# Two mixer streams in one steady interleave, modulation sums as a third stream, and low parts moved from GpSimd to VectorE

## The reference, cut to what matters

```python
for l in range(DEPTH):                                   # DEPTH = 2
    mod = cond @ ada_w[l] + ada_b[l]                     # six vectors of 1024
    sh1, sc1, g1, sh2, sc2, g2 = split(mod, 6)
    h = _rms_norm(x, norm1_g[l]) * (1.0 + sc1) + sh1
    pa, pb, pc, pd = _split(h @ w_in[l], GROUP_COLS)
    ya = _rwkv7_mixer(pa, ...)                           # recurrent state
    yb = _diff_attn_mixer(pb, ...)                       # difference of two softmaxes
    yc = _spatial_gating_mixer(pc, ...)
    yd = _forgetting_attn_mixer(pd, ...)
    x = x + g1 * (concat(ya, yb, yc, yd) @ w_out[l])
    h = _rms_norm(x, norm2_g[l]) * (1.0 + sc2) + sh2
    x = x + g2 * _conv_glu_ffn(h, ...)
# second block: gated linear attention, then
for e in range(N_EXPERTS):                               # 16 experts, each token uses 2
    he = silu(h @ w1[e]) * (h @ w3[e])
    out = out + gates[:, e:e+1] * (he @ w2[e])
return _rms_norm(x + g2 * out, final_g)
```

## Time and profile before

| | us |
|---|---|
| median of 3 runs | 2876.41 |
| lowest, highest | 2872.22, 2878.21 |
| the profiled execution: its own time | 2878.19 |
| its span in the trace | 2876.4 |
| PE busy | 2417.7 (84%) |
| DVE busy | 1581.7 (55%) |
| ACT busy | 1084.5 (38%) |
| POOL busy | 330.5 (11%) |

### The profile page before, as it was taken

One profiled execution on the slowest core, in us unless ns is written; L12 is line 12 of the kernel. 1 busy time (PEld: TensorE's weight loads), 2 busy tenths in 40 slices (PEclk: granted clock), 3 DMA queues, 4 the chain that ended last, 5 costly groups with the idle time before them and its releaser, 6 DMA issues. The chain is left out here.

```text
span 2876.4 us, 32840 instructions
## 1 busy us (share of the span) xinstructions
PE 2417.7 (84%) x11740; PEld 1931.5 (67%) x11740; DVE 1581.7 (55%) x2250; ACT 1084.5 (38%) x1633; POOL 330.5 (11%) x255
## 2 busy tenths in 40 slices
PE   2998687799989799868879998969978885789894
PEld 1777575588868577656558886847866764677773
DVE  4554656355555365566535555531446634688885
ACT  2342234233331243323433333132224322677773
POOL 0001100000000000010000000000001002566663
PEclk9996899899999799889989998969978996899997
DMA  6550000122234264000012223322570000999994
GB/s 240 189 176 4 1 30 16 59 95 93 89 117 146 84 208 143 1 1 30 30 56 93 93 80 143 131 71 74 197 241 1 1 30 31 357 348 356 360 353 168
DMA packets 94922, 354.89 MB, mean 123 GB/s; under 512 B 12736, under 2 KB 14416, under 8 KB 92496
## 3 DMA queue, kind: packets, MB, share of 16 engines
q1 hardware_dynamic: 87344, 329.16, 32.6%
q0 software_dynamic: 4288, 14.69, 1.5%
q10 hardware_dynamic: 3168, 9.45, 0.8%
HBM read 339.60 MB, written 22.04 MB: 126 GB/s over the span
## 5 line engine op out<-in xcount | busy, mean ns | idle before, releaser
L474 PE MATMUL ps<-a_hi,w_hi 128*128 128x512 f32 x1408 | 568.5, 404 | 79.8 <-PEq L324 58.0
L476 PE MATMUL ps<-a_hi,w_lo 128*128 128x512 f32 x1408 | 563.6, 400 | 0.0
L475 PE MATMUL ps<-h_lo,w_hi 128*128 128x512 f32 x1280 | 503.4, 393 | 0.0
L435 DVE TENSOR_TENSOR w_lo<-ring,w_hi 128x1024 fp32r<-128x1024 f32 x184 | 225.0, 1225 | 493.6 <-ACT w_hi L430 493.6
L430 ACT ACTIVATE w_hi<-ring 128x1024 fp32r<-128x1024 f32 x184 | 194.5, 1059 | 587.6 <-PE ps L476 574.5
L474 PEld LDWEIGHTS ps<-a_hi,w_hi 128*128 128x128 f32 x1408 | 268.2, 190 | 148.1 <-issue 65.9
L476 PEld LDWEIGHTS ps<-a_hi,w_lo 128*128 128x128 f32 x1408 | 267.3, 190 | 65.8
L475 PEld LDWEIGHTS ps<-h_lo,w_hi 128*128 128x128 f32 x1280 | 243.2, 190 | 61.9 <-issue 2.9
L2726 DVE TENSOR_TENSOR moe_w_lo<-p,moe_w_hi 128x1024 fp32r<-128x1024 f32 x144 | 240.4, 1704 | 68.7 <-ACT moe_w_hi L2824 68.1
L2824 ACT ACTIVATE moe_w_hi<-p 128x1024 fp32r<-128x1024 f32 x216 | 228.6, 1062 | 101.3 <-PE ps L2767 101.1
L2726 POOL TENSOR_TENSOR moe_w_lo<-p,moe_w_hi 128x1024 fp32r<-128x1024 f32 x72 | 180.9, 2513 | 147.6 <-ACT moe_w_hi L2824 147.6
(11 more groups left out here) (584 smaller groups left out, 4595.1 us busy)
## 6 DMA issues: line engine op xcount, KB each, us to landing
ring<-in_ffn_up SPq DMA_DIRECT2D x88, 512.0 KB, 3.4
p<-in_moe_gate SPq DMA_DIRECT2D x72, 512.0 KB, 6.0
p<-in_moe_up SPq DMA_DIRECT2D x72, 512.0 KB, 7.3
p<-in_moe_down SPq DMA_DIRECT2D x72, 512.0 KB, 5.8
vt<-in_ada SPq DMA_DIRECT2D x64, 512.0 KB, 3.8
ring<-in_w_in SPq DMA_DIRECT2D x48, 512.0 KB, 4.6
ring<-in_ffn_down SPq DMA_DIRECT2D x16, 1408.0 KB, 6.5
p<-in_ada SPq DMA_DIRECT2D x32, 512.0 KB, 4.9
```

The source lines that it names most:

```text
L435: self.c.nc.vector.tensor_tensor(self.c.w_lo[:, s % 2, :], self.c.slot(s), self.c.w_hi[:, s % 2, :].bitcast(F32), ALU.subtract).then_inc(s ...
L474: nc.tensor.matmul(bank, c.w_hi[:, s % 2, at], hi(kt), start=(kt == 0), stop=False)
L475: nc.tensor.matmul(bank, c.w_hi[:, s % 2, at], lo(kt), start=False, stop=False)
L476: ins = nc.tensor.matmul(bank, c.w_lo[:, s % 2, at], hi(kt), start=False, stop=(kt == KT - 1))
```

## The change

1. `finish_sums` and `finish_bias` leave the attention stream. A third stream, `modulation_stream`, gives PE the 32 products in four steps of eight (quarters 2, 0, 1, 3), each of which raises the semaphore; DVE adds the bias in the fourth step, for which it now waits for a count of four.
2. The plan of the mixers becomes: shift; attention's first step (empty on PE); then `1, 1, 2, 2, 1, 2, 2, 1`, which is the whole first `prepare` of the recurrent stream with the four modulation steps in it; then one `alternate` of all 45 steps of attention over the 83 left of the recurrent stream.
3. In the experts DVE makes the low parts of chunks 2, 8 and 11 too. POOL keeps chunk 5, `choose` and `gather`.

```diff
-    def sums(pe):
+    def sums(pe, parts=None):
         for m, (_, acc) in enumerate(ada.sums):
-            for t in range(n):
-                last = nc.tensor.matmul(c.ps[:, bank + m, t:t + 1], acc[t // KT][:, t % KT * P:(t % KT + 1) * P],
-                                        c.const("ones", 1), start=True, stop=True)
+            for j in parts or range(ada.count):
+                for t in range(j * KT, (j + 1) * KT):
+                    last = nc.tensor.matmul(c.ps[:, bank + m, t:t + 1], acc[j][:, t % KT * P:(t % KT + 1) * P],
+                                            c.const("ones", 1), start=True, stop=True)
         last.then_inc(summed, 1)
...
+def modulation_stream(c, name, sums, bank, quarters_in_order):
...
+    def pe():
+        for j in quarters_in_order:
+            finish_sums(nc.tensor, parts=[j])
+            yield
...
+    def dve():
+        for j in quarters_in_order:
+            if j == quarters_in_order[-1]:
+                finish_bias(nc.vector, parts=len(quarters_in_order))
+            yield
...
-    plan = [0] + [1] * b["shift"]
-    plan += alternate(a["gating"] + a["prepare"], b["prepare"] + b["intra"])
-    plan += alternate(a["forget"], b["prepare"] + b["intra"])
-    plan += alternate(a["diff"], b["scan"] + b["end"])
-    streams = [att, rw]
+    plan = [1] * b["shift"] + [0] * a["first"] + [1, 1, 2, 2, 1, 2, 2, 1]
+    plan += alternate(a["gating"] + a["prepare"] + a["forget"] + a["diff"],
+                      b["intra"] + b["prepare"] + b["intra"] + b["scan"] + b["end"])
+    streams = [att, rw, modulation]
...
             def body(i, j, r):
-                subtract_chunk(pool, nc.gpsimd, 2, j)
                 choose(i, j + 2)
                 pool.wait_ge(now, j + 3)
                 subtract_chunk(pool, nc.gpsimd, 5, j)
                 gather(i)
-                if not first(j):
-                    subtract_chunk(pool, nc.gpsimd, 8, j - 1)
-                    subtract_chunk(pool, nc.gpsimd, 11, j - 1)
...
-                lower(j, (0, 1, 3))
+                lower(j, (0, 1, 2, 3))
...
                 lower(j, (4, 6, 7))
                 if not first(j):
-                    lower(j - 1, (9, 10))
+                    lower(j - 1, (8, 9, 10, 11))
```

More of the change, by code:

```diff
@@ L279, in adaln_finish_parts, with bias @@
     n = ada.count * KT
-    def sums(pe):
+    def sums(pe, parts=None):
         for m, (_, acc) in enumerate(ada.sums):
-            for t in range(n):
-                last = nc.tensor.matmul(c.ps[:, bank + m, t:t + 1], acc[t // KT][:, t % KT * P:(t % KT + 1) * P],
-                                        c.const("ones", 1), start=True, stop=True)
+            for j in parts or range(ada.count):
+                for t in range(j * KT, (j + 1) * KT):
+                    last = nc.tensor.matmul(c.ps[:, bank + m, t:t + 1], acc[j][:, t % KT * P:(t % KT + 1) * P],
+                                            c.const("ones", 1), start=True, stop=True)
         last.then_inc(summed, 1)
-    def bias(dve):
+    def bias(dve, parts=1):
         dve.wait_ge(ada.bias, 16 * len(ada.dsts))
-        dve.wait_ge(summed, 1)
+        dve.wait_ge(summed, parts)
         for m, dst in enumerate(ada.dsts):
@@ L626, in attention_stream @@
                                       "turned", "copied", "summed", "squared", "ms", "rs", "out")}
-    finish_sums, finish_bias = adaln_finish_parts(c, "mod", sums, bank=A_BANK + 3)
     g_w = SC(3)
@@ L727, in pe @@
         eng = nc.tensor
-        finish_sums(eng)
         yield
@@ L961, in dve @@
         yield
-        finish_bias(eng)
         yield
@@ L1664, in _, with act @@
                 early(t)
+def modulation_stream(c, name, sums, bank, quarters_in_order):
+    nc = c.nc
+    finish_sums, finish_bias = adaln_finish_parts(c, name, sums, bank=bank)
+    def pe():
+        for j in quarters_in_order:
+            finish_sums(nc.tensor, parts=[j])
+            yield
+    def act():
+        for j in quarters_in_order:
+            yield
+    def dve():
+        for j in quarters_in_order:
+            if j == quarters_in_order[-1]:
+                finish_bias(nc.vector, parts=len(quarters_in_order))
+            yield
+    return dict(pe=pe, act=act, dve=dve, steps=len(quarters_in_order))
 def mixers(c, sums, w_out):
     nc = c.nc
+    modulation = modulation_stream(c, "mod", sums, A_BANK + 3, (2, 0, 1, 3))
     att = attention_stream(c, sums, nc)
@@ L1685, in _ @@
         def _(pool):
-            run("pool", streams, [0, 1, 0, 1, 0, 1, 0])
+            run("pool", streams[:2], [0, 1, 0, 1, 0, 1, 0])
         @block.tensor
@@ L2906, in _ @@
             end, more = loop(pool, body)
-            subtract_chunk(pool, nc.gpsimd, 8, end)
-            subtract_chunk(pool, nc.gpsimd, 11, end)
             for i in range(2):
@@ L2969, in _ @@
             lower_he(1, end)
-            lower(end, (9, 10))
+            lower(end, (8, 9, 10, 11))
             take_o(1, end, more)
```

## The result

| | before | after |
|---|---|---|
| median, us | 2874.61 | 2831.66 |
| lowest, highest, us | 2872.22, 2878.21 | 2826.52, 2837.30 |
| the profiled execution | 2878.19 | 2826.52 |
| its span | 2876.4 | 2824.7 |

The ratio of after to before is 0.985 (95% interval 0.9827 to 0.9873): 43 us less. The forecast was 2832, in a range of 2816 to 2864.

A forecast was written before the change was run, and what follows sets the result against it. PE, busy 84% of the span, was taken as the bound, with time saved only where it waits or runs slower. Experts 32 + modulation 10 + shares 3 = 45 off 2878.2, 2833, adjusted to the median 2832; range 2816 to 2864.

The forecast's parts named there:

- Chunk 2 and the lead: Experts: without POOL's chunk 2, DVE's low part 3 takes 1.23, and chunk 4's starts 0.35 ahead of POOL's chunk 5.
- Period: Experts: a block takes 18.6 us instead of a mean of 20.63; 15 periods gain 30.5.
- The ends of the stage: End of the experts: chunk 8's low part takes 1.23 on DVE instead of 2.36 on POOL, 1.1 gained.
- POOL's 8 and 11: Experts: these low parts become added DVE work, ahead of `product` and `lower_x`, which PE needs some 2.5 us later.
- DMA: Experts' loads: 7.22 MB a block at 18.6 is 388 GB/s, costed at nothing.
- Mixers: Both mixer layers: modulation's sums moved for 10 and equal shares for 3.
- modulation: Mixers: sums moved off the front gain 5.3 in layer 1, 3.0 in layer 2; 10 taken, ends 5 to 25.
- shares: Mixers: attention steps spread evenly change PE's waits at L811; bounds +12 and -22 for both layers, 3 taken.
- rival (d): Mixers: slower, PE waits 1.5 at each moved unit, 22 lost; 2887 together with (a) in full; chance 0.08.
- (a): Experts: POOL's chunk 5 goes first, period 20.2 to 20.8; 2862 in all blocks, 2847 in half; chance 0.25.
- (b): Experts: DMA becomes the bound at 357 GB/s, period stays at 20.2, 2856; chance 0.05.
- (c): Mixers: equal shares bring up to 12 more and the sums up to 15 more, 2815; chance 0.07.

The follow-up runs named there:

- the extra operation and all twelve: Kernel after with all twelve low parts on DVE, plus one unread DVE operation ahead of chunk 4's low part: 2826.50 us.
- all twelve: Kernel after with chunk 5's low part on DVE too, so DVE makes all twelve low parts of a block: 2819.06 us.
- mixers alone: Kernel before with both changes of the mixers and the old experts: 2864.18 us, ratio 0.996.
- extra behind 7: Kernel after with one more DVE operation a block, unread, behind chunk 7's low part: 2838.64 us.
- idle op on POOL: All twelve low parts on DVE, with POOL doing an unneeded subtraction of the same size at chunk 5's time: 2845.65 us.
- extra ahead of 4: Kernel after with one more DVE operation a block, unread, right ahead of chunk 4's low part: 2864.89 us.
- old sections: Modulation as third stream, but attention steps beside the same recurrent steps as before: 2864.59 us with the old experts, 2819.13 with all twelve low parts on DVE.
- modulation alone: Kernel before with the modulation's sums as third stream inside the first prepare, no equal shares, old experts: 2864.59 us, ratio 0.9961.

## Why the prediction was right, by its steps

**Chunk 2 and the lead.** Right in each number: chunk 3's low part 1.23; a lead of 0.35 forecast and 0.37 measured; POOL's end 2.26 behind DVE's. The Trainium skill, page "SBUF — State Buffer", section "Who interferes with whom", has the rule that I had drawn from the rows: a DVE instruction with two SBUF inputs contends with a GpSimd instruction that reads SBUF, the port pair that they share is an exclusive lock, and the order of issue decides who blocks. The traces agree (3.11 for 2.40 when POOL comes second, 2.11 for 1.23 when DVE does, and the extra of 0.6 us that turns the one into the other); the order of the starts on record is not quite that of issue, as the leads of 0.00 to -0.06 show.

**Period.** 18.6 forecast, 18.47 measured. The wait for POOL's chunk 5 is 0.3 and not 0.5, and `choose` costs DVE nothing (0.19 at 2587.02, inside DVE's run of low parts). The 15 full periods give 15 x (20.61 - 18.47) = 32.1, against 30.5. Four of the periods before were 21.8, since PE's granted clock had fallen behind the 2 us wait; no period after is.

**The ends of the stage.** Forecast 1.1, measured 36.4 - 32.1 = 4.3: this is the term of the experts that was mis-sized. The chain before shows the reason, at the last block's products after POOL's chunk 8, start and duration; then the same place after:

```profile
2828.57 2.36 POOL moe_w_lo L2726
2831.07 0.77 PE ps L2765
...
2836.53 0.43 PE ps L2765
```

```profile
2779.16 1.24 DVE moe_w_lo L2746
2780.53 0.47 PE ps L2785
...
2783.87 0.43 PE ps L2787
2784.30 0.34 PE ps L2785
```

POOL's 2.36 has become 1.24, which I had counted. But PE's wait is shorter with it (2.98 instead of 4.15), and its products run at 1.2 GHz (0.43 apart instead of 0.23) for 3.8 us after, where before it was some 6. From the last `lower_he` (2827.8 and 2778.5) to the end of the span it is 48.6 before and 46.2 after, 2.4 less. The last interval between blocks, which is short of a full period, gives 0.8, the first one 0.2, and the first block with its gather the rest, some 0.9.

**POOL's 8 and 11** I had costed as added work for DVE only. Moving them besides chunk 2 brought 34.8 - 30.5 = 4.3 us more. The intervals of the two ratios overlap, but the traces have 2.6 us of it in the 17 blocks (18.48 against 18.66) and 1.1 behind them. So the pair is worth moving beside chunk 2, though hardly alone (1.7 us, interval to zero).

**DMA.** Costed at nothing, rightly: the trace after has 397 GB/s over 200 us, and the kernel with the extra operation and all twelve 404. The Trainium skill, page "DMA: Bandwidth & Descriptors", section "Where 436 GB/s comes from", would have the HBM side bind at about 358 GB/s, and these traces don't agree. The figure of 425 for a core alone in its section "Measured (HBM→SBUF, 128 partitions, SWDGE, issued from GpSimd)" isn't contradicted.

**Mixers.** The sum, 13, was near the measured 12.4, but in part by luck. The split was wrong: modulation 10 and shares 3 forecast, 12.0 and nothing to speak of measured. And so was the way to the 10. I had 5.3 us won at the end of the first `intra` product in layer 1 and 3.0 in layer 2; the traces have 10.7 and 7.9 there, ahead of the mixers set equal. Most of the difference is the clock. I let the gating keep its 9.7 us and the second half of the product its 3.0 when they moved, but behind the first half PE ran at 2.4 GHz: 5.25, and 2.0. Then some of it was lost again, which I hadn't costed: 6.0 and 6.6 are left at the ends of the two layers. The waits at the units of forgetting rose from 22.1 to 24.5 in layer 1 and from 22.5 to 24.9 in layer 2, as rival (d) had it, at about a fifth of that rival's price (4.8 of 22), and PE's granted clock from 310 to 345 us was 0.66 instead of 0.76. The rest of the loss wasn't taken apart. ACT's table load (1.28 us) did leave the path, but ACT now waits 2.4 us for POOL's memset of `h` in its place, and PE 3.95 for ACT (1.05 before). The shares' 3 was a choice between bounds of +12 and -22 with no row that spoke for it.

**The mixers' gain comes or stays away with the clock.** This I hadn't seen. Between the same products ahead of the mixers and behind them, layer 1 gained 6.0 to 6.3 us in five executions with both parts (after, mixers alone, extra behind 7, all twelve, idle op on POOL) and -0.2 in two (extra ahead of 4, and that with all twelve); layer 2 gained 5.5 to 6.6 in three and -0.1 in four. Nothing lies between. With the old sections layer 1 gained 2.7 once and 12.1 once. The stages that gained nothing, and the one with 2.7, have a stretch at 1.2 GHz ahead of their end that the others lack: from 465 to 480 us the granted clock is 0.66 in those three of layer 1, and 1.00 in the five that gained 6.0 to 6.3. Two windows from the end of layer 2's mixers, first after, then after with the extra behind chunk 7 (length, busy PE, PEld, DVE, ACT, POOL, PEclk, DMA share, GB/s):

```profile
1380.00:1383.00 3.00, 3.00 (x33) 2.73 (x31) 1.77 (x8) 1.83 (x5) 0.00 (x0) 1.00 0.01 3
...
1386.00:1389.00 3.00, 3.00 (x38) 2.63 (x37) 0.45 (x2) 0.22 (x1) 0.00 (x0) 1.00 0.00 0
```

```profile
1380.00:1383.00 3.00, 3.00 (x33) 2.68 (x30) 1.75 (x9) 1.83 (x5) 0.00 (x0) 1.00 0.01 3
...
1386.00:1389.00 3.00, 3.00 (x21) 2.66 (x20) 0.22 (x1) 0.45 (x2) 0.00 (x0) 0.50 0.00 0
```

Up to 1384 the two executions agree within 0.05 us; both then have PE waiting 1.38 us for a unit of differential attention, and behind that wait one has 2.4 GHz and the other 1.2 GHz for some 14 us. What decides it I don't know: the instructions of the stage are the same. It is at least a part of why single executions of one kernel lie up to 20 us apart (modulation alone: 2853.14 to 2873.06), and it is why I lean on medians for the mixers and on the traces for the experts.

**What the rivals came to.** (a), POOL first, did not happen, but was one 0.6 us operation away: forced, it gave 2864.9 with both parts of the mixers in, where I had 2862. What I had held against it, that a lost block leaves DVE ahead in the next, is true of the one block lost with the extra behind chunk 7, and false with the extra ahead of chunk 4: 16 blocks in a row were lost. (b) fell with 397 GB/s. (c) and (d) both rested on the shares, which are worth nothing measurable.

## What to carry to other kernels

When two engines share a resource that one instruction holds to its end, look at who starts first at each meeting and by how much: here one instruction moved away turned 2.2 us of waiting a block into 0.3, and 0.6 us of work put in the wrong place gave it all back. A slow helper engine is not free help even where nobody waits for its results: taking the last subtraction from POOL, which left DVE with more work, made the stage as fast as PE itself. When a stretch of matmuls moves, its price is that of the clock at its new place: the gating took 9.7 us at 1.2 GHz and 5.25 at 2.4. A gain that depends on the clock after a short wait has to be judged by several executions, not by one trace.

## What the hardware showed that I had not expected

- POOL's subtraction that nobody needs costs 26.6 us in the run and 1.7 in a steady block, most of its own 2.4. It doesn't always get in behind the DVE operation that it met: once DVE made six low parts first, and POOL's took 8.88.
- At a meeting, POOL's record may start 0.06 ahead of DVE's and DVE still goes first (13 blocks with 0.00 to 0.06); at 0.065 ahead (one block) and at 0.24 (16 blocks) POOL does.
- PE can be kept busy for 200.00 of 200 us with fp32 weights streamed in at 397 GB/s.
- Identical instructions behind the same wait of 1.38 us got 2.4 GHz in one execution and 1.2 GHz in another, 5.5 to 6.6 us a stage.
